# Gate matrix of a mixture layer: ScalarE's gelu and next high part moved ahead of its gate copy, the gelu split four tokens lower, VectorE's small product moved ahead of its big one

## The reference

```python
def block(t):
    q = (t @ w_pq).reshape(T, PEER_HEADS, 2, PEER_HALF)
    s = jnp.einsum('thpk,hpnk->thpn', q, sub_keys)
    # the 16 best pairs of sub-keys per head: experts = i1 * 128 + i2, gate = softmax(best scores)
    u = expert_down[experts]
    act = jax.nn.gelu(jnp.einsum('td,thkd->thk', t, u), approximate=False)
    wgt = gate * act
    vv = expert_up[experts]
    return jnp.einsum('thk,thkd->td', wgt, vv)
```

## Time and profile before

| | us |
|---|---|
| timed runs | 3096.58, 3090.17, 3094.7 |
| median | 3094.7 |
| profiled execution | 3090.84 |
| its span | 3089.0 |
| TensorE busy (matmuls) | 2923.0 (95%) |
| VectorE busy | 2269.7 (73%) |
| ScalarE busy | 1470.8 (48%) |
| GpSimd busy | 741.7 (24%) |

### The profile page before, as it was taken

How to read it: one execution, slowest core, us unless ns; L and a number is a source line. 1 busy time by engine, 2 the same in 40 slices (tenths; PEclk the granted TensorE clock), 3 DMA queues, 4 the chain that set the end, 5 groups by cost and what they waited for, 6 DMA issues and landing times. The chain is left out here.

```text
span 3089.0 us, 49236 instructions
## 1 busy us (share of the span) xinstructions
PE 2923.0 (95%) x19366; PEld 2674.2 (87%) x19366; DVE 2269.7 (73%) x4037; ACT 1470.8 (48%) x2425; POOL 741.7 (24%) x374
## 2 busy tenths in 40 slices
PE   6999998999999988999998999999899999999998
PEld 5788988888898877899998988887799999988887
DVE  4868996686799767697568677777689657756665
ACT  3344433434433344445665445554454665545454
POOL 0100000010000001488776100001079776400000
PEclk8999999999999999999999999999899999999999
DMA  6434554553455453454443777784345443455554
GB/s 193 173 130 170 205 199 156 189 178 135 157 198 212 170 187 112 151 178 164 142 139 120 250 263 260 274 297 137 110 158 185 145 142 130 162 180 194 194 192 162
DMA packets 125976, 547.96 MB, mean 177 GB/s; under 512 B 13715, under 2 KB 17972, under 8 KB 101300
## 3 DMA queue, kind: packets, MB, share of 16 engines
q1 hardware_dynamic: 125604, 544.30, 51.3%
q10 hardware_dynamic: 144, 0.52, 0.0%
HBM read 538.48 MB, written 6.29 MB: 176 GB/s over the span
## 5 line engine op out<-in xcount | busy, mean ns | idle before, releaser
L2008 POOL TENSOR_TENSOR q_lo<-q_raw,q_hi 128x1024 fp32r<-128x1024 f32 x250 | 677.9, 2722 | 226.9 <-ACT q_hi L2117 226.5
L2027 PE MATMUL k_psN<-k_hhi,q_hi 128*128 128x256 f32 x2304 | 665.6, 289 | 18.9 <-POOL q_lo L2008 18.0
L2027 PE MATMUL k_psN<-k_hhi,q_lo 128*128 128x256 f32 x2304 | 651.5, 283 | 0.0
L2027 PE MATMUL k_psN<-k_hlo,q_hi 128*128 128x256 f32 x2304 | 651.4, 283 | 0.0
L2117 ACT ACTIVATE q_hi<-q_raw 128x1024 fp32r<-128x1024 f32 x538 | 566.4, 1053 | 5.6 <-DMA q_raw<-up 3.1
L741 DVE TENSOR_TENSOR k_wlo<-k_raw,k_whi 128x2048 fp32r<-128x2048 f32 x158 | 360.5, 2286 | 150.6 <-ACT k_whi L568 150.5
L2027 PEld LDWEIGHTS k_psN<-k_hhi,q_hi 128*128 128x128 f32 x2304 | 441.1, 191 | 25.9 <-POOL q_lo L2008 21.8
L2320 DVE TENSOR_TENSOR q_lo<-q_raw,q_hi 128x1024 fp32r<-128x1024 f32 x288 | 352.8, 1225 | 130.5 <-ACT q_hi L2117 129.9
L2027 PEld LDWEIGHTS k_psN<-k_hlo,q_hi 128*128 128x128 f32 x2304 | 441.6, 192 | 0.0
L2027 PEld LDWEIGHTS k_psN<-k_hhi,q_lo 128*128 128x128 f32 x2304 | 441.0, 191 | 0.0
L568 ACT ACTIVATE k_whi<-k_raw 128x2048 fp32r<-128x2048 f32 x158 | 301.1, 1911 | 244.1 <-PE f_psA L420 98.9
(11 more groups left out here) (355 smaller groups left out, 5483.6 us busy)
## 6 DMA issues: line engine op xcount, KB each, us to landing
k_raw<-ws SPq DMA_DIRECT2D x180, 1024.0 KB, 4.8
q_raw<-down SPq DMA_DIRECT2D x288, 512.0 KB, 3.4
q_raw<-up SPq DMA_DIRECT2D x256, 512.0 KB, 3.5
k_x<-ada SPq DMA_DIRECT2D x48, 512.0 KB, 3.6
e_ada<-ada SPq DMA_DIRECT2D x48, 512.0 KB, 4.9
out<-k_x SPq DMA_DIRECT2D x3, 1024.0 KB, 3.9
k_x<-out SPq DMA_DIRECT2D x3, 1024.0 KB, 6.2
k_x<-x SPq DMA_DIRECT2D x2, 1024.0 KB, 5.9
```

The lines of the kernel that those rows point to most:

```text
L2008: nc.gpsimd.tensor_tensor(lo[:, i % RING, :], raw[:, i % RING, :], hi[:, i % RING, :].bitcast(F32), ALU.subtract).then_inc(S["lo_pool"], 1)
L2027: last = nc.tensor.matmul(psD(n), w, h, start=kt == 0 and i == 0, stop=kt == KT - 1 and i == 2)
```

## The change

Nothing is computed otherwise and no instruction is added or taken away. Three things move.

- `gelu_tiles(g)` is FIRST + g and not FIRST + g - 1 (from group 1 on): the big product of a group covers one unit more, the gate copy one less. It now waits for the gelu of unit 45+g-1, which was one earlier before.
- `gates_before(j)` is 4 (j + 1) and not 4 (j + 2): the small product of a unit covers four tokens fewer.
- In ScalarE's turn gelu pair and high part stand first, then hot row and gate copy. In VectorE's turn the small product of j = g-3 stands ahead of the big product of g-2. The call of `rest` that issued nothing is gone.

```diff
 def gelu_tiles(g):
-    return FIRST + max(0, g - 1)
+    return FIRST + g
...
 def gates_before(j):
-    return min(T, GROUP * (j + 2))
+    return min(T, GROUP * (j + 1))
...
                 for g in range(GROUPS):
-                    if g + 2 < GROUPS:
-                        gated_last(g + 2)
-                    to_a(g)
                     if g:
                         n = PQ + FIRST + g - 1
                         take(n)
                         head(n + RING)
+                    if g + 2 < GROUPS:
+                        gated_last(g + 2)
+                    to_a(g)
...
                     if g < GROUPS:
                         gated(g)
+                    if g >= 3:
+                        gate_early(g - 3)
                     if 2 <= g < GROUPS + 2:
                         into_a(g - 2)
-                    if g >= 3:
-                        gate_early(g - 3)
-                        rest(PQ + FIRST + g - 3 + RING)
```

## The result

The changed kernel takes 3070.98 us (median of four runs, 3067.28 to 3073.1), the kernel before 3094.76: a ratio of 0.9925, 95% interval 0.9912 to 0.9938. Forecast were 3071.5 us. Measured are 23.8 us less than before, forecast 23.2.

What follows compares the result with a forecast made beforehand. The gate stage was taken as bound by TensorE, with late low parts costing 11.6 us a layer. Removing 23.2 us for both layers from 3094.7 gave 3071.5 us, range 3065 to 3082.

Steps and rivals of the forecast that it cites:

- What bounds the stage: Gate stage: TensorE bounds its first 152 us; in the 98 us behind, it is busy 89.00 and waits for low parts.
- The sum: Both gate stages: 10.9 us over 62 turns plus 0.7 behind them, 11.6 a layer, 23.2 for both.
- The new turn: Gate stage: gelu and high part start earlier, subtraction 1.50 us behind the unit's end, hot copies held every turn without loss.
- Pairs cost time only through the gate copy ahead of the high part: Gate stage: paired turns (5.02 and 3.76 us) cost TensorE time only because ScalarE's high part stands behind the gate copy.
- a wait that goes, at no gain: VectorE: with the small product first, its wait on ScalarE between the products goes; the big one is due as today.
- The loop of before: VectorE and GpSimd exclude each other: small product, hot copies, compare and subtraction take about 3.8 us against TensorE's 3.77.
- The cover: Gate stage: GpSimd's low part is ready 4.3 us before TensorE needs it, against 2.2 in the present order.
- some of the loss stays: Rival, chance 0.10: hand-overs in VectorE and GpSimd's loop cost 0.3 us more, 7.7 us a layer lost, around 3087.
- The slower rival: Rival, chance 0.06: the subtraction beats VectorE's small product, the gate copy slips, turns take 4.39 us from the start, 3150.
- The walk: VectorE and GpSimd, followed from the undisturbed turn at 1520: new loop 3.60 to 3.78 us, within 3.767 in nearly all turns.

Runs made afterwards that it cites:

- Run 2: Kernel before with only VectorE's small product moved, a turn later and ahead of the big one; ScalarE's order and split as before: 3072.99 us, ratio 0.9926.
- Run 1: Changed kernel with VectorE's order put back (big product, then small product), keeping ScalarE's new order and the split: 3074.2 us, ratio 0.993.
- run 5: Changed kernel with all four hot copies of a group on VectorE, without ScalarE's two activations for the fourth: 3108.82 us, ratio 1.0054.
- run 6: Changed kernel with picked keys' transposes and ScalarE's Exp one unit earlier, its first two hot rows ahead of the last plain gelu: 3084.63 us, ratio 0.9972.
- run 9: Kernel before with the small product a turn later, ahead of the big one, and the picked keys' transposes one unit earlier: 3090.09 us, ratio 0.999.
- Run 4: Changed kernel with ScalarE's high part ahead of the gelu pair: 3137.27 us, ratio 1.0137.
- run 8: Changed kernel with gate copy and small product a turn later, and the picked keys' transposes one unit earlier: 3063.11 us, ratio 0.99.

## Why the prediction was right, and where its steps were not

**What bounds the stage: right.** TensorE's turn of 3.767 us is what is left once nobody holds it, and the second part's loss was all there was to win. 244.43 - 233.53 = 10.90 us a layer; 10.9 was forecast. The whole stage gave 11.6 in layer 1; in layer 2 a stretch at the lower clock took 1.5 back. The sum was right; that the medians meet it within 0.5 us is luck (3.5 us were lost outside the stages in the profile).

**The new turn: right.** Behind the unit's end (1659.57: its last matmul starts 0.12 before the gates' first and takes 0.28) the gelu starts at 0.04, the subtraction at 1.51 (forecast 1.50), the small product at 1.27 (1.23), the big one at 1.57 (1.4 to 1.6), and the gate copy ends at 2.43 (by 2.7). The hot copies are held in every turn as forecast. They take 2.9 us at the start of the stage and 2.43 at its end, since the products ahead of them grow and they are issued ever later behind the subtraction (0.1 us, then 0.59).

**"Pairs cost time only through the gate copy ahead of the high part": half right.** The prediction gave the gain to ScalarE's order. Run 2 keeps the old one and wins the same. What the prediction listed under VectorE as a wait that goes, at no gain, shortens the loop below TensorE's turn, and that is enough. Run 1, with ScalarE's order alone, forms pairs by group 50. And pairs have a second way to cost time: in runs 1, 5 and 6 they hold TensorE through late hot rows, while in the kernel before and run 9 it waits for low parts. Two conditions made the loss; the changed kernel's loop fits into TensorE's turn, so the first is gone.

**The loop of before: its terms are a little off.** Small product 0.2, hot copies 0.77, compare 0.68 and subtraction 2.25 make 3.9, not "about 3.8". The hot copies start 0.11 us behind the subtraction's end (it starts at 1595.72 and takes 3.04, so 1598.76 to 1598.87), not 0.2, and that gives 3.81, as measured. It exceeds 3.77 only late in the stage: at 1523.15 the small product still starts with the gelu and takes its usual 0.24 us.

**The cover: the wrong one.** The case "some of the loss stays" set GpSimd's lead of 4.3 us against a longer loop. In runs 1, 4, 5 and 6 no down unit of the stage waits for a low part, but for up to 0.08 us at the end of run 5: what runs out is the lead of the hot rows ahead of the gates. In run 5, 38 us were lost and not the 10 expected of it.

**The slower rival: real, but with one door more.** Run 4 has its mechanism at the row that it named. What the prediction didn't have is that no unlucky subtraction is needed: with the changed order itself and another start of the stage (run 6) the coupled pairs hold. The walk began from an undisturbed turn and took it for granted that the stage gets there. It did, but run 6 shows that this was not a matter of course. The price was too high, though. Run 4, built to be slower, takes 3137 us and not 3150, and run 6 with its pairs 3084.6 (without the pauses ahead of the stages). An unlucky start would thus have brought about the time before the change or a few us less, not the slower rival's time.

## What to carry to other kernels

Where two engines exclude each other and a third waits for one of them ahead of work that the other needs, add up the loop and compare it with the turn of the engine that should bound. Here a loop that outgrew that turn by 0.04 us showed only in GpSimd's pause, which shrank from 0.95 to 0.65 us, for 45 turns, and then cost 10.9 us. Look at every operand of the bounding engine for its lead, not only at the one that was late first: here low parts before the change, hot rows in the runs after it. And such a loop can run in two ways (233.53 and 244.46 us for the same 62 turns), so a version that looks worse may only have started in the wrong one: cut the wait (here, the gate copy a turn later), and gains elsewhere, such as the removed pause, come through.

## What the runs showed of the hardware

- A small product behind a running subtraction is held until that ends (2.24 us issued 0.29 behind it, 2.11 issued 0.42 behind), and three hot copies can be held by two subtractions in a row (5.02 us). A compare directly behind hot copies was never held (0.67 to 0.69 us in all stages of all twelve profiles), though a subtraction had been issued 0.15 us before it; why it goes first was not settled.
- TensorE's granted clock fell behind a short pause in some places and not in others: after 2.67 us of waiting the first turn of a stage had clock 1.00 and took 3.84 us in layer 1, and 0.69 and 5.35 us in layer 2 of the same execution. In all twelve profiles there are thirteen such pauses of 2.67 us: six were followed by 1.00, seven by 0.53 to 0.72 and a turn of 5.2 to 6.6 us. Behind the three pauses of 4.58 us it was 0.61 or 0.62 each time. With the pause gone it took 3.80 us in all six stages of the profiles of runs 6, 8 and 9.
